# State updates of four batch elements on 32-row tiles of TensorE, in four PSUM banks

## What is computed

```python
p = rmsnorm(x, g_mix_pre) @ w_in          # q, k, v, o-gate, conv inputs, gates
num   = einsum('bhls,bshd->blhd', s, vc) + einsum('blhd,bhde->blhe', qc, C) * w_inter
h     = num / maximum(abs(den), exp(-m_t))
hm    = sigmoid(o) * h
C_new = g_state * C + einsum('bhs,bshd,bshe->bhde', g_keys, kc, vc)   # for each of 8 sequences
x     = x + rmsnorm(concat[hm, conv] @ w_out, g_mix_post)
```

## Time and profile before

| | us |
|---|---|
| median of 3 runs (2153.62 to 2154.33) | 2153.66 |
| the profiled execution, whole | 2154.55 |
| its span, first to last instruction | 2152.8 |
| PE busy | 2145.0 (100%) |
| PEld busy | 2134.2 (99%) |
| DVE busy | 982.1 (46%) |
| ACT busy | 891.3 (41%) |
| POOL busy | 959.4 (45%) |

### The profile page before, as it was taken

How to read it: one execution, slowest core, us unless ns; L and a number is a source line. 1 busy time by engine, 2 the same in 40 slices (tenths; PEclk the granted TensorE clock), 3 DMA queues, 4 the chain that set the end, 5 groups by cost and what they waited for, 6 DMA issues and landing times.

```text
span 2152.8 us, 41799 instructions
## 1 busy us (share of the span) xinstructions
PE 2145.0 (100%) x16248; PEld 2134.2 (99%) x16248; DVE 982.1 (46%) x1422; ACT 891.3 (41%) x1151; POOL 959.4 (45%) x563
## 2 busy tenths in 40 slices
PE   9999999999999999999999999999999999999998
PEld 9999999999999999999999999999999999999998
DVE  6533432223434324987769738543432223333323
ACT  6434333334343335644345446434333333333443
POOL 1444443434444445476756332444443334444444
PEclk9999999999999999999999999999999999999999
DMA  7454455545554554566766554555455545454653
GB/s 250 165 169 162 164 168 169 163 161 172 164 167 158 174 165 149 204 195 237 242 198 223 200 164 145 170 165 167 157 172 169 166 157 171 161 173 157 210 165 130
DMA packets 121860, 377.69 MB, mean 175 GB/s; under 512 B 28552, under 2 KB 33804, under 8 KB 120496
## 3 DMA queue, kind: packets, MB, share of 16 engines
q1 hardware_dynamic: 97632, 349.00, 49.2%
q10 hardware_dynamic: 24016, 27.42, 4.0%
q0 software_dynamic: 128, 0.07, 0.0%
HBM read 361.26 MB, written 15.18 MB: 175 GB/s over the span
## 4 chain that ended last, share of the span: by engine, by line
PE 99%; DVE 0%; DMA 0%; SPq 0%; ACT 0%; issue 0%
PE bank L484 30%; PE bank L482 30%; PE bank L483 30%; PE bank L537 1%; PE bank L544 1%; PE bank L548 1%; PE bank L826 1%; PE bank L828 1%; PE bank L827 1%; PE bank L748 0%; PE bank L707 0%; DMA raw<-stream 0%; PE bank L689 0%; DVE x_res L1416 0%; DVE bank L1415 0%; PE bank L732 0%
## 5 line engine op out<-in xcount | busy, mean ns | idle before, releaser
L1864 POOL TENSOR_TENSOR wlo<-raw,whi 128x1024 fp32r<-128x1024 f32 x331 | 794.5, 2402 | 851.8 <-ACT whi L898 771.9
L482 PE MATMUL bank<-xh,whi 128*128 128x288 f32 x3344 | 992.2, 297 | 0.0
L483 PE MATMUL bank<-xl,whi 128*128 128x288 f32 x3344 | 988.3, 296 | 0.0
L484 PE MATMUL bank<-xh,wlo 128*128 128x288 f32 x3344 | 986.4, 295 | 0.0
L898 ACT ACTIVATE whi<-raw 128x1024 fp32r<-128x1024 f32 x652 | 687.3, 1056 | 597.6 <-PE bank L484 555.1
L1317 DVE TENSOR_TENSOR wlo<-raw,whi 128x1024 fp32r<-128x1024 f32 x323 | 469.4, 1455 | 769.5 <-ACT whi L898 768.2
L482 PEld LDWEIGHTS bank<-xh,whi 128*128 128x128 f32 x3344 | 630.2, 188 | 2.4 <-issue 2.2
L484 PEld LDWEIGHTS bank<-xh,wlo 128*128 128x128 f32 x3344 | 629.7, 188 | 0.0
L483 PEld LDWEIGHTS bank<-xl,whi 128*128 128x128 f32 x3344 | 628.7, 188 | 0.2
L484 PE MATMUL bank<-hh,wlo 128*128 128x288 f32 x1408 | 417.4, 296 | 0.0
L482 PE MATMUL bank<-hh,whi 128*128 128x288 f32 x1408 | 416.1, 296 | 0.0
(11 more groups left out here) (262 smaller groups left out, 1264.1 us busy)
## 6 DMA issues: line engine op xcount, KB each, us to landing
raw<-stream SPq DMA_DIRECT2D x654, 512.0 KB, 3.6
C<-c_in ACTq DMA_DIRECT2D x4, 2048.0 KB, 8.8
cs_out<-C ACTq DMA_DIRECT2D x4, 2048.0 KB, 8.9
y_out<-x_res SPq DMA_DIRECT2D x7, 288.0 KB, 2.8
bc<-row_copy ACTq DMA_DIRECT2D x4, 448.0 KB, 8.9
conv_out<-upad ACTq DMA_DIRECT2D x4, 302.0 KB, 5.5
upad<-conv_in ACTq DMA_DIRECT2D x4, 272.0 KB, 3.8
vtok<-turned_v ACTq DMA_DIRECT2D x8, 128.0 KB, 3.1
```

What stands on the lines that cost most here:

```text
L482: pe.matmul(out, wh, mov_hi[:, k, :], start=first, stop=False)
L483: pe.matmul(out, wh, mov_lo[:, k, :], start=False, stop=False)
L484: return pe.matmul(out, wl, mov_hi[:, k, :], start=False, stop=last)
L1864: pool.tensor_tensor(wlo[:, g % SLOTS, :], raw[:, g % SLOTS, :], whi[:, g % SLOTS, :].bitcast(F32), ALU.subtract).then_inc(lo_ready[g % SL ...
```

## The change

The four copies of a decode token now stand next to each other (rows are 8 sequences x 4 copies x 4 tokens), so that the 16 rows of a sequence lie together and two sequences fill a group of 32 rows. A matmul of the update contracts over 32 rows only: `tile_position=(NS * g, 0)` puts it on one of four row tiles of PE, and each tile writes a bank of its own (7, 4, 5, 6). `vm` has two masked copies instead of eight. Instead of eight calls a head there are two, at (k - `LATE[h]`, j) = (17,1) and (18,3), each with eight matmuls, for four sequences. The second waits until DVE has evicted the four results of the first.

Banks 5 and 6 hold the head's output until then. So for heads 0 to 2 ACT copies it to `heads` in SBUF (two copies in step k = 16 + `LATE`), and the gate works from there, in place on `qkvo[:, 3]`; the first update call waits for these copies (`heads_kept`). For the last head nothing is copied: its first update call waits for `mix_ready` of that head. The layout also needs other masks (`low8`, `low16`, `side`, `colv`, made once), four instead of two copies into `kv4`, and two full-height instructions instead of three partial ones for the low parts.

```diff
+PAR = NB // Q_GROUP
+COPIES = P // NS
+UPDATE_ORDER = (0, 2, 4, 6, 1, 3, 5, 7)
+UPDATE_BANK = (7, 4, 5, 6)
...
+        heads = place("heads", [P, D_MLSTM // P, TOK], F32, arena[0])
...
-        vm = place("vm", [P, NB, DH], F32R)
+        vm = place("vm", [P, PAR, DH], F32R, vm_at)
...
+        def copied(ap):
+
+            return ap.unsqueeze(2).broadcast_to([ap.shape[0], NB, COPIES, NT])
+
+        def in_copies(ap):
+
+            return ap.rearrange("p (b j t) -> p b j t", j=COPIES, t=NT)
+
+        def gated_head(h, e):
+            return qkvo[:, 3, e, :] if h < H - 1 else bank[5 + e][:, 0:TOK]
...
-                                           C[:, r * Q_GROUP + j, c, :], start=(r + c == 0),
+                                           C[:, PAR * j + r, c, :], start=(r + c == 0),
...
-                    pe.wait_ge(mix_ready, 2 * h)
+                    pe.wait_ge(cu_evicted, NB * h)
...
-            def update_memory(h, b):
-
-                if b < 2:
-                    pe.wait_ge(den_ready if b == 0 else qc_evicted, h + 1)
+            def update_memory(h, n):
+
+                if n:
+                    pe.wait_ge(cu_evicted, NB * h + Q_GROUP)
                 else:
-                    pe.wait_ge(cu_evicted, NB * h + b - 1)
-                pe.wait_ge(vm_ready, NB * h + b + 1)
-                out = bank[4 if b % 2 else 7]
+                    pe.wait_ge(den_ready, h + 1)
+                    pe.wait_ge(qc_evicted, h + 1)
+                    pe.wait_ge(vm_ready, PAR * (h + 1))
+                    if h < H - 1:
+                        pe.wait_ge(heads_kept, DC * (h + 1))
+                    else:
+                        pe.wait_ge(mix_ready, DC * H)
                 for c in range(DC):
-                    mm = pe.matmul(out[:, c * DH:(c + 1) * DH], k4[:, c * P:(c + 1) * P], vm[:, b, :],
-                                   start=True, stop=True)
-                mm.then_inc(cu_done, 1)
+                    for g in range(Q_GROUP):
+                        own_rows = slice(NS * g, NS * (g + 1))
+                        mm = pe.matmul(bank[UPDATE_BANK[g]][:, c * DH:(c + 1) * DH], k4[own_rows, c * P:(c + 1) * P],
+                                       vm[own_rows, n, :], start=True, stop=True, tile_position=(NS * g, 0))
+                        if c == DC - 1:
+                            mm.then_inc(cu_done, 1)
...
-            updates = {(16, 1): 0, (16, 4): 1, (16, 7): 2, (17, 2): 3, (17, 5): 4, (18, 0): 5, (18, 3): 6, (18, 6): 7}
+            updates = {(17, 1): 0, (18, 3): 1}
 
             def between(p, j):
 
@@ -791,9 +819,9 @@
                         denominators(h)
                     if (k, j) == ATTEND_AT[h]:
                         attend(h)
-                    b = updates.get((k - LATE[h], j))
-                    if b is not None:
-                        update_memory(h, b)
+                    n = updates.get((k - LATE[h], j))
+                    if n is not None:
+                        update_memory(h, n)
...
-                act.dma_start(row_copy[:, R_GK:ROWS], rowg[:, 0:TOK]).then_inc(rows_stored, 16)
+                act.dma_start(row_copy[:, R_GK:R_GK + SEQ], rowg[:, 0:SEQ]).then_inc(rows_stored, 16)
+                act.dma_start(row_copy[:, R_GK + SEQ:ROWS].rearrange("h (b t) -> h b t", t=NT),
+                              in_copies(rowg[:, SEQ:SEQ + P])[:, :, 0, :]).then_inc(rows_stored, 16)
...
-                        last = act.activation(kv4[:, n, :, :].rearrange("p c (j t) -> p c j t", j=P // NS),
-                                              four(qkvo[:, 1 + n, :, SEQ:TOK]), ACT.Copy)
+                        for c in range(DC):
+                            last = act.activation(in_copies(kv4[:, n, c, :]), copied(
+                                qkvo[:, 1 + n, c, SEQ:TOK].rearrange("p (b t) -> p b t", t=NT)), ACT.Copy)
...
-                    act.activation(v4[:, :], bank[7][:, 0:DH], ACT.Copy, scale=col[:, 5, h:h + 1])
-                    act.activation(k4[:, :], bank[7][:, DH:2 * DH], ACT.Copy).then_inc(dec_hi, 1)
+                    act.wait_ge(colv_ready, 1)
+                    act.activation(v4[:, :], bank[7][:, 0:DH], ACT.Copy, scale=colv[:, 1, h:h + 1])
+                    act.activation(k4[:, :], bank[7][:, DH:2 * DH], ACT.Copy, scale=side[:, 1, 0:1]).then_inc(dec_hi, 1)
...
-                if k in (12, 13):
+                if k == 12:
 
                     act.wait_ge(dec_lo, h + 1)
                     act.wait_ge(mask_ready, 1)
-                    for b in range(4 * (k - 12), 4 * (k - 11)):
-                        act.activation(vm[:, b, :], v4[:, :].bitcast(F32), ACT.Copy, scale=mask[:, b:b + 1])\
+                    for r in range(PAR):
+                        act.activation(vm[:, r, :], v4[:, :].bitcast(F32), ACT.Copy, scale=mask[:, r:r + 1])\
                            .then_inc(vm_ready, 1)
+                if k == 16 + LATE[h] and h < H - 1:
+                    for e in range(DC):
+                        act.wait_ge(num_done, 3 * h + 2 + e)
+                        act.activation(heads[:, DC * h + e, :], bank[5 + e][:, 0:TOK], ACT.Copy).then_inc(heads_kept, 1)
...
-                        act.wait_ge(hm_ready, 2 * h)
+                        act.wait_ge(mix_ready, 2 * h)
...
-                        act.activation(mh[:, h * DC + e, :], bank[5 + e][:, 0:TOK], ACT.Copy).then_inc(hm_hi, 1)
+                        act.activation(mh[:, h * DC + e, :], gated_head(h, e), ACT.Copy).then_inc(hm_hi, 1)
...
+            dve.wait_ge(low_ready, 2)
+            dve.tensor_reduce(side[:, 0, 0:1], low16[:, :], AX_X, ALU.add)
+            link(dve.tensor_reduce(side[:, 0, 1:2], low8[:, :], AX_X, ALU.add))
+            dve.tensor_scalar(side[:, 1, :], side[:, 0, :], -2.0, 1.0, ALU.mult, ALU.add).then_inc(side_ready, 1)
...
+                    dve.wait_ge(side_ready, 1)
+                    for n in range(2):
+                        last = dve.tensor_scalar(colv[:, n, :], col[:, 5, :], side[:, n, 1:2], None, ALU.mult)
+                    last.then_inc(colv_ready, 1)
+                    dve.wait_ge(colv_ready, 1)
...
-                    for r in (NS, 3 * NS):
-                        dve.scalar_tensor_tensor(out=v4[r:r + NS, :], in0=bank[7][r:r + NS, 0:DH],
-                                                 scalar=col[r:r + NS, 5, h:h + 1], in1=v4[r:r + NS, :].bitcast(F32),
-                                                 op0=ALU.mult, op1=ALU.subtract)
-                    half = slice(2 * NS, P)
-                    dve.tensor_tensor(k4[half, :], bank[7][half, DH:2 * DH], k4[half, :].bitcast(F32), ALU.subtract)\
-                       .then_inc(dec_lo, 1)
+                    dve.scalar_tensor_tensor(out=v4[:, :], in0=bank[7][:, 0:DH], scalar=colv[:, 0, h:h + 1],
+                                             in1=v4[:, :].bitcast(F32), op0=ALU.mult, op1=ALU.add)
+                    dve.scalar_tensor_tensor(out=k4[:, :], in0=bank[7][:, DH:2 * DH], scalar=side[:, 0, 0:1],
+                                             in1=k4[:, :].bitcast(F32), op0=ALU.mult, op1=ALU.add).then_inc(dec_lo, 1)
...
-                for b in ((0, 1, 2), (3, 4), (5, 6, 7))[first] if 0 <= first < 3 else ():
-                    dve.wait_ge(cu_done, NB * h + b + 1)
-                    src = bank[4 if b % 2 else 7][:, :]
+                for n in range(4 * first - 4, 4 * first) if 1 <= first < 3 else ():
+                    dve.wait_ge(cu_done, NB * h + n + 1)
+                    b = UPDATE_ORDER[n]
+                    src = bank[UPDATE_BANK[b // PAR]][:, :]
...
-                        dve.wait_ge(num_done, 3 * h + 3)
                         dve.wait_ge(ro_ready, 2 * h + e + 1)
-                        head = bank[5 + e][:, 0:TOK]
-                        dve.tensor_tensor(head, head, qkvo[:, 3, e, :], ALU.mult).then_inc(hm_ready, 1)
+                        if late:
+                            dve.wait_ge(num_done, 3 * H)
+                            head = bank[5 + e][:, 0:TOK]
+                        else:
+                            dve.wait_ge(heads_kept, DC * h + e + 1)
+                            head = heads[:, DC * h + e, :]
+                        dve.tensor_tensor(gated_head(h, e), head, qkvo[:, 3, e, :], ALU.mult).then_inc(hm_ready, 1)
                 if o in ((7,) if late else (6, 8)):
                     for e in (0, 1) if late else (o // 2 - 3,):
                         dve.wait_ge(hm_hi, 2 * h + e + 1)
-                        dve.tensor_tensor(ml[:, h * DC + e, :], bank[5 + e][:, 0:TOK],
+                        dve.tensor_tensor(ml[:, h * DC + e, :], gated_head(h, e),
...
+            for low, n in ((low8, 4), (low16, 8)):
+                pool.memset(low[:, :], 1.0).then_inc(pool_chain, 1)
+            pool.wait_ge(pool_chain, 6)
```

More of the change, by code:

```diff
@@ L256, in hybrid_layer_kernel @@
         assert gwt_at + 4 * XC * GATE_M <= vm_at + 4 * NB * DH
-        vm = place("vm", [P, NB, DH], F32R)
+        vm = place("vm", [P, PAR, DH], F32R, vm_at)
```

(38 more changed lines are left out.)

52 lines of the change are left out of this document (20 added, 32 removed).

## The result

| | before | after |
|---|---|---|
| median, us | 2153.75 (14 runs) | 2157.82 (14 runs) |
| lowest to highest, us | 2153.62 to 2154.6 | 2157.16 to 2161.71 |
| profiled span, us | 2152.8 | 2156.3 |

The ratio is 1.002, 95% interval 1.0012 to 1.0027: slower by 4.1 us. The forecast was 2152.7 with a range up to 2156.0, so it was wrong, and on the side of a loss.

A forecast was written before the change was run, and what follows sets the result against it. PE, busy 2145.0 of 2152.8 us, was taken as the bound. Terms -7.7 (removed) + 5.3 (added) + 1.4 (last-head wait) = -1.0 us, so the median 2153.66 becomes 2152.7, range 2150.5 to 2156.0.

The forecast's parts named there:

- Removed from PE, 7.7: PE's stream loses 64 update matmuls in 32 pairs, 0.24 us a pair: 7.7 us less.
- added, 5.3: PE gains eight row-tiled update calls of eight matmuls, 0.66 us each: 5.3 us more.
- B: Row tiles' weight loads in the update calls come one after another: +4.2 us, 2157.9; chance 0.10.
- D: PE changes over to row tiles for nothing in the update calls: -4.4 us, 2149.3; chance 0.04.
- E: Row tiles' matmuls in the update calls run one after another too: +4.7 us, 2158.4; chance 0.03.
- The wait in the last head, 1.4: PE waits at the last head's first update call for mh and ml, behind ACT's four DMA issues: 1.4 us.
- the lower bound that I named: Last head: without the one long DMA issue, all is 1.1 us earlier and PE's wait 0.2 us.
- The second call's evictions: A head's second update call waits for DVE's four evictions, ready 3.34 us after the first call's start; margin 1.3 us.
- rival C: DVE's evictions before the second update call come late, 0.4 us over the margin: 2154.5; chance 0.08.
- Edits at nothing: New masks, side, colv, kv4 copies, v4 and k4 work, head copies and stored-row transfers were priced at no time.
- the cover that I quoted: Head 1: DVE's low keys ready at 999.79, PE asks at 1006.32, so 6.5 us of cover.
- Something I did not cost: Whole kernel: chance 0.06 for an effect outside the forecast and its rivals, with no size given.

The follow-up runs named there:

- experiment 7: Changed kernel with the gate on a PSUM operand and colv from PSUM, plus each update call's eight matmuls issued twice: 2154.5 us, 1.4 more than without.
- experiment 2: Changed kernel with the two small VectorE instructions for colv reading the columns in PSUM, not their SBUF copy: 2157.41 us.

## Why the prediction was wrong

- **Removed from PE, 7.7, and added, 5.3**: right. Tiles run side by side, 0.64 us a call for 0.66, 5.1 in all. Rivals B, D and E are out by the trace, B and E by experiment 7 as well.
- **The wait in the last head, 1.4**: mechanism right, size off. It was 0.3. ACT's rows in answer to the earlier trace rows:

```profile
1204.82 2.67 ACTq L1145 DMA_DIRECT2D turned_k<-qkvo  x4
1207.53 0.72 ACT L1242 ACTIVATE mh<-bank 128x288 fp32r<-128x288 f32 x2 [1.68 <-issue]
```

  The four issues took 2.67, the lower bound that I named (3.79 less 1.1), not the row of before.
- **The second call's evictions** (rival C): right that they are no bound for the second call. DVE's four took 2.72 us and ended 3.2 us after the call's start, where I had 3.34, and PE's waits name none for C:

```profile
1209.45 2.72 DVE L1786 SCALAR_TENSOR_TENSOR C<-C,bc,bank 128x512 f32<-128x512 f32 x4 [0.65 <-PE bank L775]
```

  Behind the last call the four do cost 0.3 us: DVE's next split begins at 1216.72, 3.7 us later than before, where PE is 3.1 us later, and what DVE owes PE there comes later too. This is read from the rows and not tested.
- **Edits at nothing**: this step failed, twice. First, the gate of heads 0 to 2 from SBUF is not in the sum and not among the edits at nothing. Leaving it out gave the SBUF form the durations of the PSUM form. With POOL running, 12 instructions that took 0.45 us each took 1.57 (products) and 1.14 (`ml`) on average, 10.8 us more of DVE in heads 0 to 2, worth 4.3 us at the end. `colv` was named and priced at nothing, and cost 3.60 us of DVE and 0.7 us of time.
- Second, the cover that I quoted was the wrong one. 6.5 us lay before the scores, but the first reader of a late DVE is the transposes, with 0.8 us in hand in the last head. Between the gate and the transposes DVE works through the taps of the convolution (L1651) without a gap, so nothing there absorbs a delay.
- The trace of before held the warning. DVE's splits (L1317), with two SBUF inputs, took 1.16 to 2.84 us with a median of 1.23. The 96 of 323 that began while POOL's split had over 0.4 us to go took 1.63 to 2.84, the others at most 1.55. `qwn`, 32 columns, took 2.34 us at 928.73, where POOL's split began at 928.65. I read the durations of the lines that the change kept and not the spread of lines with the operands that it was about to use.
- "Something I did not cost" had 0.06. It was this, and the range had left a part of it out.

When DVE comes first, POOL is held. In the changed kernel, DVE and then POOL:

```profile
1216.72 1.22 DVE L1353 TENSOR_TENSOR wlo<-raw,whi 128x1024 fp32r<-128x1024 f32 x1
...
1217.08 3.12 POOL L1913 TENSOR_TENSOR wlo<-raw,whi 128x1024 fp32r<-128x1024 f32 x1 [8.42 <-ACT whi L926]
```

POOL's splits between 950 and 1200 us were 2.42 us on average in the changed kernel and 2.40 with the gate on PSUM, so little of it falls on POOL there. What stays open: what sets, from one execution to the next, which of the two comes first, and whether the clock falls after the wait.

## What to carry to other kernels

Moving an operand of VectorE from PSUM to SBUF is not neutral: with both inputs in SBUF, it waited here for the rest of GpSimd's split, up to the whole of it (2.70 us for 0.44). Look at GpSimd's row for the same stretch before pricing such an edit, and keep one input in PSUM if GpSimd is busy. Read the max of a line and not only its median: a min and max that are far apart in the kernel before name the collision. For a delay on an engine, ask for the smallest slack among all who read from it, in order of time. And count a wait of TensorE by the starts of its matmuls before and behind it, not by the wait alone: here 2.3 us of waiting were 4.1 us, with the clock.

## What the runs showed of the hardware

- VectorE, product or difference of 128 x 288 with two SBUF inputs: 0.44 us alone, up to 2.70 beside GpSimd's 2.42 us instruction, up to 1.55 beside one of 1.30. With one PSUM input it was at most 0.467 in every kernel. The place of the output did not matter.
- The other way round, GpSimd's split took 3.12 us for 2.40 when VectorE's, with two SBUF inputs, had begun 0.36 us before it.
- A product with one SBUF tensor and a per-partition SBUF scalar (128 x 4) was held as well, 1.8 us each; from PSUM 0.22.
- Four row tiles of 32 rows ran side by side, loads too. Going over to them and back cost 0.4 us a call; a further group of four matmuls with 256 columns, 0.12.
- TensorE's granted clock was 0.50 after an idle stretch of 2.3 us in the changed kernel's trace, at a cost of 1.6 us, and stayed 1.00 after one of the same length in that of experiment 2.
